# The opening of a two-block transformer kernel: the order of its modulation units, first key blocks and context squares

## The chip, the cores and the metric

The kernel runs on one core of a Trainium2 chip. The core has five engines that run their own programs and wait for each other through semaphores: TensorE (PE: matmuls; its weight loads are shown apart as PEld), VectorE (DVE), ScalarE (ACT), GpSimd (POOL) and SyncE (SP, which here issues every DMA but one). The metric is the device time of one execution in microseconds (us); lower is better.

## What is computed

The reference applies a first block of two layers (a grouped-query attention layer with a context, then a neighbourhood attention layer), and a second block (an mLSTM branch and a sparse attention branch, merged). The change touches the start of the first layer alone:

```python
mod_x = (silu_c @ w_mod[i] + b_mod[i])[:, None, :]
mod_c = silu_cc @ w_mod[i] + b_mod[i]
sh_x, sc_x, g_x = jnp.split(mod_x, 3, axis=-1)
sh_c, sc_c, g_c = jnp.split(mod_c, 3, axis=-1)
hx = rms_norm(x, norm_g[i]) * (1.0 + sc_x) + sh_x
hc = rms_norm(ctx, norm_g[i]) * (1.0 + sc_c) + sh_c
...
k = px[..., A_WIDTH:A_WIDTH + A_KV_WIDTH].reshape(b, t, A_KV_HEADS, HEAD_DIM)
pkv = hc @ w_in[:, A_WIDTH:A_WIDTH + 2 * A_KV_WIDTH]
```

x has 512 tokens and ctx 256, both of width 1024. Everything is float32 and is kept to near that precision: each operand of a projection is split into a high part and a low part (its rest), and each product is three matmuls (high by high, high by low, low by high).

## The kernel before

**Layout.** Activations lie transposed, in eight blocks of 128 features (k = 0 to 7): 512 columns of x and 256 of the context each. HX and LX are the high and low parts of x after norm and modulation, HC and LC those of the context, WH and WL those of the weights. Weights come in units of 1 MB; a unit has four quarters of 512 columns, and quarter q serves the blocks k = 2q and 2q + 1.

**Order.** A Python list, `plan`, is filled in program order by `do(...)`. Every engine then walks the same list and emits its own share of each item, so each engine runs strictly in the list's order, and moving a line in the opening moves it on all engines at once. There is no scheduler in the part that is changed; the order is written by hand, and `opening[0] = True` keeps the projections from putting weight splits between themselves.

**Modulation units.** Shift and scale of the first layer come from eight units, 0 to 3 (shift) and 4 to 7 (scale). `EARLY` gives their order of loading: 0, 4, 1, 5, 2, 6, 3, 7; this text calls them e0 to e7 in that order, and `first[n]` is the generator of en. `next(first[n])` puts three things into the list: the 8 matmuls of the unit (`mod_mm`, L1722, 16 in the trace), and ACT's copy of their sum out of PSUM (`mod_row`, L1998). `run(first[n])` puts the rest: two transposes on PE (`mod_tr`, L1730) and the small DVE operations (L2276 to L2285) that make the shift, or for e1, e3, e5 and e7 the gain. e(2j) and e(2j+1) together serve the blocks k = 2j and 2j + 1. Four buffers hold the loaded units: the load of e(n+4) waits for the matmuls of en (L2882).

**Per block of x.** `scale(k)` is DVE's product of x, gain and norm factor (L2327, into AR) and then ACT's addition of the shift, rounded to HX (L2022). `scale_low(k)` is DVE's rest, LX (L2333). `keys_rows(0, [k])` is the six matmuls of 512 columns of block k (L1704 to L1706). They wait for LX of that block and the WL quarter.

**Context.** `square("a", k, 1)` squares block k of the context on ACT (L2009) and adds it on DVE (L2294); `norm_sums` sums over the partitions on PE (L1740); `norm_rs` is DVE's mean (L2300) and POOL's power (L2763); `rbroad` is DVE's diagonal (L2315) and PE's broadcast (L1747); `scale_ctx` is ACT's copy of the broadcast factors, Rc (L2015). From there `ctx_normed(k)` is POOL's product with Rc (L2775), `ctx_rows_in(k)` is two ACT operations (L2030, HC, and L2032, the same in full) and POOL's rest LC (L2780), and `keys_rows(1, ks)` the matmuls of 256 columns on the context's blocks.

**Weight splits.** `tick(True)` puts one quarter's split into the list: ACT's cast to WH (L1991) and POOL's rest WL (L2756), or DVE's (L2268) for unit 1. After the fourth quarter follows the load of the unit after next.

**Fillers.** `busy(n)` issues n matmuls on constants into an unused bank (L1713, two passes each in the trace). Their result is read by nobody.

Of the kernel before, what the change touches and what calls it, by code (L numbers as in the profile page):

```python
# [172 lines left out]
def build(nc, wu, vp, cc, cs1, xt, biasb, pos, out):  # L173
    ctx = ExitStack()
    with ctx:
# [152 lines left out]
        def do(*item):  # L328
            plan.append(item)
            done_work[0] += COST.get(item[0], 0)  # L330
# [12 lines left out]
        def run(g):  # L343
            for _ in g:
                pass
# [5 lines left out]
        def load(n):  # L351
            if n < len(UNITS):
                loaded.add(n)
                loaded_at[n] = done_work[0]
                do("load", n)
# [8 lines left out]
        def tick(forced=False):  # L364


            if opening[0] and not forced:
                return
            if pieces and (forced or not careful[0] or done_work[0] - loaded_at[pieces[0][0]] > 9):
                n, q = pieces.pop(0)  # L370
                split_by[n, q] = "pool" if n != 1 and not quick[0] else "dve"
                do("split", n, q)
                if q == 3:
                    load(n + 2)
                split_ready()

        def split_ready():
            for m in sorted(loaded):
                if UNITS[m][0] not in PLAIN and m not in started and part_last[PART[m]] in (None, *unit_end):
                    split(m)  # L380
# [29 lines left out]
        def pj(key, un, lo, hi, f0, phase, o, ks=range(8), half=None):  # L410

            groups[key] = Group(key, un.n, False, lo, hi, f0, 128, phase, o, half)
            for k in ks:
                if k % 4 == 3:
                    tick()
                do("proj", key, k)
                yield (hi - lo) / (100 if half is None else 200)
# [35 lines left out]
        def early_unit(n, pr):  # L453
            w = early[n % 4].rearrange("p (k f) -> p k f", k=8)
            return mod_unit(0, EARLY[n], pr, w, (s_early[n % 4], (n,)), lambda: None)
# [35 lines left out]
        def rbroad(name, p, o):  # L491
            rbout[name, p] = o
            for i in range(*norms[name].parts[p]):
                dg_prev[name, i], dg_last[i % 4] = dg_last[i % 4], (name, i)
                do("rbroad", name, i)
# [53 lines left out]
        first = [early_unit(n, FIRST if n < 2 else MODS) for n in range(8)]  # L549
        modulate(0, PS[:, 0:1024], "a", False, hb0, "a", ())  # L550

        def keys_rows(j, ks):
            lo, hi = FULL[j]
            for m in range(2):
                run(pj(("ak", m, j), un, lo, hi, 128 * m, "a", K4[m][:, lo:hi], ks))

        def ctx_rows_in(*ks):
            for k in ks:
                do("low_ctx_k", 0, k)

        def ctx_normed(*ks):
            for k in ks:
                do("norm_ctx_k", 0, k)

        def scale(*ks):
            for k in ks:
                do("scale", 0, k)

        def scale_low(*ks):
            for k in ks:  # L570
                do("scale_low", 0, k)
# [20 lines left out]
        tick(True)  # L592
        scale(0, 1)
        scale_low(0, 1)
        do("busy", 3)
        next(first[2])
        do("busy", 3)
        tick(True)
        for k in range(4, 8):
            do("square", "a", k, 1)  # L600
        keys_rows(0, [0])
        next(first[3])
        keys_rows(0, [1])
        tick(True)
        tick(True)
        run(first[2])
        run(first[3])
        do("norm_sums", "a", 1)
        do("norm_rs", "a", 1)

        next(first[4])
        scale(2, 3)
        next(first[5])
        rbroad("a", 1, PS[:, 0:1024])
        do("scale_ctx", 0)
        ctx_normed(0, 1, 2, 3)
        scale_low(2, 3)
        run(first[4])
        run(first[5])
        keys_rows(0, [2, 3])  # L620
        ctx_rows_in(0, 1)

        scale(4)
        next(first[6])
        scale(5)
        next(first[7])
        ctx_normed(4, 5)
        scale_low(4, 5)
        keys_rows(0, [4])
        run(first[6])  # L630
        run(first[7])
        ctx_rows_in(2, 3)
        keys_rows(0, [5])
        keys_rows(1, [0, 1])

        scale(6, 7)
        ctx_normed(6, 7)
        scale_low(6, 7)
        opening[0] = False
# [536 lines left out]
        first = [(s_post, ("b", 31)), (s_gated, ("b", 7))]  # L1176
# [301 lines left out]
        def hidden(m, blocks, pr):  # L1478

            un = Unit("w1" + "kv"[m])  # L1480
            w1[m] = (un.n, bank(pr.take(("w1", m), (s_hid, (m,)))))
            for i, n in enumerate(blocks):
                for x in range(n):
                    do("n_hidden", m, sum(blocks[:i]) + x)
                yield
            un.done(s_hidp, m)
# [47 lines left out]
        hv, first = hidden(1, [0, 0, 0] + [2] * 8, SEVEN), first_probs()  # L1534
# [1566 lines left out]
```

## Time and profile before

| | us |
|---|---|
| median of 3 executions | 1564.93 |
| their range | 1561.18 to 5181.44 |
| the profiled execution | 1565.51 |
| its span in the trace | 1563.5 |

| engine | busy us | share of the span |
|---|---|---|
| PE | 1512.9 | 97% |
| PE weight loads | 1226.5 | 78% |
| DVE | 755.4 | 48% |
| POOL | 688.3 | 44% |
| ACT | 645.7 | 41% |

Times in the trace count from the start of the span. A line of the timeline gives the start, the busy time of the instructions merged into it, the engine, the source line, what is written and read, the shapes and the count; in brackets how long the engine was idle before it and what released it. A busy PE is not PE at its peak, since matmuls are pipelined and their ends are modelled. The first 60 us are the stage of the change.

### The profile page before, as it was taken

What the parts mean: (1) busy time and instruction counts of PE and PEld (TensorE: products, weight loads), DVE (VectorE), ACT (ScalarE), POOL (GpSimd) and SP (SyncE); (2) the same over time, 40 slices, a digit from 0 to 9 for tenths busy, and PEclk for the clock granted to TensorE, in tenths of its full rate; (3) what the DMA queues carried; (4) which work ended last, traced back from release to release, by engine and by line L of the source; (5) the groups of instructions that cost most, each with busy time, mean ns of one, the idle gap of its engine ahead of it and who ended that gap; (6) DMA issues with size and microseconds to landing.
All of it is one profiled execution on the core that took longest, in us unless ns stands there. A gap on an engine that the chain in (4) does not pass through costs nothing.

```text
span 1563.5 us, 25447 instructions
## 1 busy us (share of the span) xinstructions
PE 1512.9 (97%) x10072; PEld 1226.5 (78%) x10072; DVE 755.4 (48%) x1675; ACT 645.7 (41%) x1393; POOL 688.3 (44%) x661
## 2 busy tenths in 40 slices
PE   7999999999899999999998999999999999999997
PEld 4877777777687888787876896878787877777887
DVE  5344545445534344435455765734443564555154
ACT  5345444444532533333334553445333334444331
POOL 3444444444532533433434535445355435554462
PEclk9999999999999999999999999999999999999999
DMA  9211111121033222322221322122131231111221
GB/s 394 77 55 55 55 55 37 56 72 54 1 109 108 82 81 82 108 82 82 85 105 34 129 88 81 59 87 98 54 108 55 85 105 55 54 55 55 84 91 67
DMA packets 23285, 128.22 MB, mean 82 GB/s; under 512 B 2432, under 2 KB 4736, under 8 KB 9216
## 3 DMA queue, kind: packets, MB, share of 16 engines
q1 hardware_dynamic: 23024, 126.35, 23.0%
q8 instruction: 80, 1.31, 0.3%
q10 hardware_dynamic: 144, 0.26, 0.1%
q14 instruction: 37, 0.30, 0.1%
HBM read 124.50 MB, written 2.10 MB: 81 GB/s over the span
## 4 chain that ended last, share of the span: by engine, by line
PE 85%; DVE 4%; ACT 4%; POOL 3%; issue 2%; DMA 1%; SPq 0%; POOLq 0%; DVEq 0%; ACTq 0%
PE PS L1704 17%; PE PS L1706 16%; PE PS L1705 16%; PE PS L1800 7%; PE PS L1790 7%; PE PS L1826 6%; PE PS L1696 3%; PE PS L1697 3%; PE PS L1698 3%; POOL WL L2756 1%; PE PS L1722 1%; PE PS L1883 1%; PE PS L1875 1%; DVE sm L2416 1%; ACT WH L1991 1%
## 5 line engine op out<-in xcount | busy, mean ns | idle before, releaser
L2756 POOL TENSOR_TENSOR WL<-W,WH 128x512 fp32r<-128x512 f32 x307 | 411.1, 1353 | 329.5 <-ACT WH L1991 329.4
L1704 PE MATMUL PS<-HX,WH 128*128 128x512 f32 (+1 forms) x1032 | 414.3, 401 | 8.0 <-POOL WL L2756 5.1
L1706 PE MATMUL PS<-HX,WL 128*128 128x512 f32 (+1 forms) x1032 | 393.5, 381 | 0.0
L1705 PE MATMUL PS<-LX,WH 128*128 128x512 f32 (+1 forms) x1032 | 393.5, 381 | 0.0
L1704 PEld LDWEIGHTS PS<-HX,WH 128*128 128x128 f32 x1032 | 196.2, 190 | 55.0 <-issue 17.5
L1706 PEld LDWEIGHTS PS<-HX,WL 128*128 128x128 f32 x1032 | 195.8, 190 | 38.5
L1705 PEld LDWEIGHTS PS<-LX,WH 128*128 128x128 f32 x1032 | 196.6, 191 | 32.3 <-issue 2.6
L2815 POOL TENSOR_SCALAR AR<-AR,sm 128x768 f32<-128x768 f32 (+4 forms) x160 | 112.6, 708 | 248.1 <-DVE sm L2435 246.4
L1991 ACT CAST WH<-W 128x512 fp32r<-128x512 f32 x320 | 187.9, 621 | 36.9 <-DMA W<-in_wu 13.6
L2416 DVE TENSOR_REDUCE sm<-PS 128x1 f32<-128x512 f32 (+4 forms) x192 | 145.0, 755 | 55.1 <-PE PS L1790 51.2
L2077 ACT ACTIVATE AR<-PS,sm 128x768 f32<-128x768 f32 (+4 forms) x160 | 114.9, 722 | 104.3 <-DVE sm L2421 86.1
L2088 ACT COPY AR<-PS 128x512 f32<-128x512 f32 (+1 forms) x112 | 62.2, 555 | 154.3 <-PE PS L1800 154.1
L1790 PE MATMUL PS<-AR 64*128 64x256 f32 (+3 forms) x704 | 119.1, 453 | 4.7 <-ACT AR L2077 1.7
L2815 POOL TENSOR_SCALAR XC<-XC,sm 128x512 f32<-128x512 f32 x64 | 45.3, 708 | 160.4 <-DVE sm L2435 160.4
L1704 PE MATMUL PS<-HC,WH 128*128 128x256 f32 (+1 forms) x344 | 108.8, 316 | 1.0 <-POOL LC L2780 1.0
L2077 ACT ACTIVATE XC<-PS,sm 128x512 f32<-128x512 f32 x64 | 44.1, 690 | 146.1 <-DVE sm L2421 146.1
L1706 PE MATMUL PS<-HC,WL 128*128 128x256 f32 (+1 forms) x344 | 103.3, 300 | 0.0
L1800 PE MATMUL PS<-C,AR 128*128 128x128 f32 x608 | 95.7, 281 | 4.4 <-DVE AR L2455 3.1
L1790 PEld LDWEIGHTS PS<-AR 64*128 64x128 f32 x704 | 59.6, 186 | 49.4 <-issue 38.1
L1826 PEld LDWEIGHTS PS<-AR 128*64 128x64 f32 x1408 | 76.2, 137 | 28.2 <-issue 24.7
L1826 PE MATMUL PS<-AR 128*64 128x128 f32 x1408 | 93.6, 279 | 4.3 <-DVE AR L2444 2.5
L1696 PE MATMUL PS<-WH,HX 128*128 128x256 f32 x320 | 94.0, 294 | 0.0
(284 smaller groups left out, 2507.1 us busy)
## 6 DMA issues: line engine op xcount, KB each, us to landing
W<-in_wu SPq DMA_DIRECT2D x98, 1024.0 KB, 4.8
AR<-in_wu SPq DMA_DIRECT2D x8, 1024.0 KB, 10.0
AR<-in_biasb SPq DMA_DIRECT2D x32, 256.0 KB, 2.8
XX<-in_xt SPq DMA_DIRECT2D x2, 1024.0 KB, 6.3
XC<-in_xt SPq DMA_DIRECT2D x1, 1024.0 KB, 12.8
out<-XX SPq DMA_DIRECT2D x2, 512.0 KB, 3.0
out<-XX SPq DMA_DIRECT2D x4, 256.0 KB, 2.2
C<-in_cc SPq DMA_DIRECT2D x1, 642.5 KB, 11.1
```

The lines of the kernel that those rows point to most:

```text
L1696: e.matmul(o, xh, wh, start=(k == 0), stop=False)
L1704: e.matmul(o, wh, xh, start=(k == 0), stop=False)
L1705: e.matmul(o, wh, xl, start=False, stop=False)
L1706: t = e.matmul(o, wl, xh, start=False, stop=(k == 7))
L1790: t = e.matmul(PS[:, s.score[h] + a:s.score[h] + b], l, r, start=True, stop=True)
L1800: t = e.transpose(o[:, j * 128:j * 128 + 128], s.pb[h][:, (q0 + j) * 128:(q0 + j) * 128 + 128], c("id"))
L1826: t = e.matmul(s.out[h][j], s.values[h][j], s.pt[h][:, j * 128:j * 128 + 128], start=(j % apart == 0 and s.first), stop=(j % apart == apar ...
L1991: e.copy(WH[:, PART[n], a:z], W[:, n % 2, a:z]).then_inc(*s_wh.by(n, q))
L2077: t = e.activation(s.pb[h][:, a:b], PS[:, s.score[h] + a:s.score[h] + b], ACT.Exp, bias=smn[:, i % 4, g:g + 1], scale=(1.0 if s.scale is N ...
L2416: e.tensor_reduce(mx, x, AX.X, ALU.max).then_inc(*s_max.by(name, n, h))
L2756: e.tensor_tensor(WL[:, d, a:z], W[:, n % 2, a:z], WH[:, d, a:z].bitcast(F32), ALU.subtract).then_inc(*s_wl_pool.by(n, q))
L2815: t = e.tensor_scalar(x, x, rin[:, i % 8, g:g + 1], 1.0 if s.gate is None else s.gate[h][:, g:g + 1], ALU.mult, ALU.mult)
```

## The change

The two groups of three fillers behind the first modulation units go. The matmuls of e3 move ahead of block 0's keys, and the transposes of e2 and e3 between the keys of block 0 and block 1. Squares of context blocks 6 and 7 move behind `scale(2, 3)`. e4 and e5 are multiplied ahead of block 2's keys, and transposed behind them. The context's sums, its power, its broadcast and Rc move behind the keys of blocks 2 and 3. Of the context's blocks, 0 and 1 are brought in between the matmuls of e6 and e7, 2 and 3 behind `scale(6, 7)`.

```diff
--- before.py
+++ after.py
@@ -592,48 +592,46 @@
         tick(True)
         scale(0, 1)
         scale_low(0, 1)
-        do("busy", 3)
         next(first[2])
-        do("busy", 3)
         tick(True)
-        for k in range(4, 8):
+        for k in range(4, 6):
             do("square", "a", k, 1)
+        next(first[3])
         keys_rows(0, [0])
-        next(first[3])
+        run(first[2])
+        run(first[3])
         keys_rows(0, [1])
+        next(first[4])
+        scale(2, 3)
+        for k in range(6, 8):
+            do("square", "a", k, 1)
+        next(first[5])
+        scale_low(2, 3)
         tick(True)
         tick(True)
-        run(first[2])
-        run(first[3])
+        keys_rows(0, [2])
+        run(first[4])
+        run(first[5])
         do("norm_sums", "a", 1)
+        keys_rows(0, [3])
+        scale(4)
         do("norm_rs", "a", 1)
-
-        next(first[4])
-        scale(2, 3)
-        next(first[5])
+        scale(5)
         rbroad("a", 1, PS[:, 0:1024])
         do("scale_ctx", 0)
         ctx_normed(0, 1, 2, 3)
-        scale_low(2, 3)
-        run(first[4])
-        run(first[5])
-        keys_rows(0, [2, 3])
+        next(first[6])
+        scale_low(4, 5)
         ctx_rows_in(0, 1)
-
-        scale(4)
-        next(first[6])
-        scale(5)
         next(first[7])
-        ctx_normed(4, 5)
-        scale_low(4, 5)
         keys_rows(0, [4])
         run(first[6])
         run(first[7])
+        ctx_normed(4, 5)
+        keys_rows(0, [5])
+        scale(6, 7)
         ctx_rows_in(2, 3)
-        keys_rows(0, [5])
         keys_rows(1, [0, 1])
-
-        scale(6, 7)
         ctx_normed(6, 7)
         scale_low(6, 7)
         opening[0] = False
```

Source lines below the change are two lower in the changed kernel (L1998 is L1996 there). The rows below are the programs of the engines in their order, each with the semaphores it waits for.

PE, from behind the transposes of e0 and e1, before: L1713 are fillers, L1722 the modulation matmuls, L1704 to L1706 the keys.

```order
L1713 MATMUL PS<-C 128x256 x3
L1722 MATMUL PS<-AR,sm 32x256 [waits early2,norm_var]
L1722 MATMUL PS<-AR,sm 32x256 x7
L1713 MATMUL PS<-C 128x256 x3
L1704 MATMUL PS<-HX,WH 128x512 [waits x_low_dve,w_low_pool,mod_gain]
L1705 MATMUL PS<-LX,WH 128x512
L1706 MATMUL PS<-HX,WL 128x512
L1704 MATMUL PS<-HX,WH 128x512
L1705 MATMUL PS<-LX,WH 128x512
L1706 MATMUL PS<-HX,WL 128x512
L1722 MATMUL PS<-AR,sm 32x256 [waits early3,mod]
L1722 MATMUL PS<-AR,sm 32x256 x7
```

The same place in the changed kernel, where L1720 are the modulation matmuls, L1702 to L1704 the keys and L1728 the transposes.

```order
L1720 MATMUL PS<-AR,sm 32x256 [waits early2,norm_var]
L1720 MATMUL PS<-AR,sm 32x256 x7
L1720 MATMUL PS<-AR,sm 32x256 [waits early3,mod]
L1720 MATMUL PS<-AR,sm 32x256 x7
L1702 MATMUL PS<-HX,WH 128x512 [waits x_low_dve,w_low_pool,mod_gain]
L1703 MATMUL PS<-LX,WH 128x512
L1704 MATMUL PS<-HX,WL 128x512
L1702 MATMUL PS<-HX,WH 128x512
L1703 MATMUL PS<-LX,WH 128x512
L1704 MATMUL PS<-HX,WL 128x512
L1728 MATMUL PS<-C,AR 128x128 [waits mod_row]
L1728 MATMUL PS<-C,AR 128x128
```

e3's matmuls stand ahead of the first six key matmuls instead of behind them, the transposes of e2 and e3 right behind these instead of behind twelve, and the fillers are gone.

ACT, from behind the cast of unit 0's second quarter, before: L2009 are squares of the context, L1998 the copies of modulation sums, L1991 the casts, L2022 the blocks of HX, L2015 is Rc.

```order
L2009 ACTIVATE AR<-XC 128x256 [waits squares_added] x4
L1998 COPY AR<-PS 128x256 [waits mod_turned,mod_sums]
L1991 CAST WH<-W 128x512 x2
L1998 COPY AR<-PS 128x256 [waits mod_turned,mod_sums]
L2022 ACTIVATE HX<-AR,sm 128x512 [waits mod,scaled]
L2022 ACTIVATE HX<-AR,sm 128x512 [waits scaled]
L1998 COPY AR<-PS 128x256 [waits mod_turned,mod_sums]
L2015 COPY AR<-PS 128x256 [waits rs_broad]
```

The same place in the changed kernel (L2020 is HX, L1989 the cast, L2013 Rc).

```order
L2007 ACTIVATE AR<-XC 128x256 [waits squares_added] x2
L1996 COPY AR<-PS 128x256 [waits mod_turned,mod_sums] x2
L2020 ACTIVATE HX<-AR,sm 128x512 [waits mod,scaled]
L2020 ACTIVATE HX<-AR,sm 128x512 [waits scaled]
L2007 ACTIVATE AR<-XC 128x256 [waits squares_added] x2
L1996 COPY AR<-PS 128x256 [waits mod_turned,mod_sums]
L1989 CAST WH<-W 128x512 x2
L2020 ACTIVATE HX<-AR,sm 128x512 [waits mod,scaled]
L2020 ACTIVATE HX<-AR,sm 128x512 [waits scaled]
L2013 COPY AR<-PS 128x256 [waits rs_broad]
```

The copies of e3's and e4's sums (the "x2") now stand directly ahead of HX of blocks 2 and 3; the squares of blocks 6 and 7, the copy of e5's sums and both casts stand behind it; HX of blocks 4 and 5 stands ahead of Rc. On DVE the additions of squares 6 and 7 stand, in the same way, between the products of blocks 2 and 3 and their LX.

ACT, from HX of block 4 on, before; a pair of L2030 and L2032 is one block of the context.

```order
L2022 ACTIVATE HX<-AR,sm 128x512 [waits mod,scaled]
L1998 COPY AR<-PS 128x256 [waits mod_turned,mod_sums]
L2022 ACTIVATE HX<-AR,sm 128x512 [waits scaled]
L1998 COPY AR<-PS 128x256 [waits mod_turned,mod_sums]
L2030 ACTIVATE HC<-AR,sm 128x256 [waits normed_ctx,mod_gain]
L2032 ACTIVATE AR<-AR,sm 128x256 [waits x_high]
L2030 ACTIVATE HC<-AR,sm 128x256 [waits normed_ctx]
L2032 ACTIVATE AR<-AR,sm 128x256 [waits x_high]
L2022 ACTIVATE HX<-AR,sm 128x512 [waits mod,scaled]
L2022 ACTIVATE HX<-AR,sm 128x512 [waits scaled]
L2030 ACTIVATE HC<-AR,sm 128x256 [waits normed_ctx,mod_gain]
L2032 ACTIVATE AR<-AR,sm 128x256 [waits x_high]
```

The changed kernel, from the copy of e7's sums on (L2020 is HX of blocks 6 and 7 here, L2028 and L2030 a block of the context).

```order
L1996 COPY AR<-PS 128x256 [waits mod_turned,mod_sums]
L2020 ACTIVATE HX<-AR,sm 128x512 [waits mod,scaled]
L2020 ACTIVATE HX<-AR,sm 128x512 [waits scaled]
L2028 ACTIVATE HC<-AR,sm 128x256 [waits normed_ctx,mod_gain]
L2030 ACTIVATE AR<-AR,sm 128x256 [waits x_high]
L2028 ACTIVATE HC<-AR,sm 128x256 [waits normed_ctx]
L2030 ACTIVATE AR<-AR,sm 128x256 [waits x_high]
L2028 ACTIVATE HC<-AR,sm 128x256 [waits normed_ctx,mod_gain]
L2030 ACTIVATE AR<-AR,sm 128x256 [waits x_high]
L2028 ACTIVATE HC<-AR,sm 128x256 [waits normed_ctx]
L2030 ACTIVATE AR<-AR,sm 128x256 [waits x_high]
```

Ahead of HX of blocks 6 and 7 before stood four blocks of the context, now two; behind it, until the last block, four before and six now.

## Rows read from the trace of the kernel before

**Rows 1.** Page: busy us, share and instructions of each engine.
```profile
PE 1512.9 (97%) x10072; PEld 1226.5 (78%) x10072; DVE 755.4 (48%) x1675; ACT 645.7 (41%) x1393; POOL 688.3 (44%) x661
```

**Rows 2.** PE in order of time, 21 to 53 us.
```profile
21.88 1.07 PE L1722 MATMUL PS<-AR,sm 128*32 128x256 f32 x16
...
26.35 1.07 PE L1722 MATMUL PS<-AR,sm 128*32 128x256 f32 x16
...
28.87 0.60 PE L1730 MATMUL PS<-C,AR 128*128 128x128 f32 x4
...
29.74 1.93 PE L1722 MATMUL PS<-AR,sm 128*32 128x256 f32 x32
32.30 0.71 PE L1747 MATMUL PS<-AR,C 128*128 128x128 f32 x4 [0.63 <-DVE AR L2315]
...
52.52 0.28 PE L1696 MATMUL PS<-WH,HX 128*128 128x256 f32 x1
```

**Rows 3.** ACT in order of time, 25 to 44 us.
```profile
25.16 0.72 ACT L2009 ACTIVATE AR<-XC 128x256 f32<-128x256 f32 x2
...
30.88 0.37 ACT L1998 COPY AR<-PS 128x256 f32<-128x256 f32 x1 [1.69 <-PE PS L1722]
31.14 1.33 ACT L2022 ACTIVATE HX<-AR,sm 128x512 fp32r<-128x512 f32 x2
...
33.05 0.37 ACT L2015 COPY AR<-PS 128x256 f32<-128x256 f32 x1 [0.31 <-PE PS L1747]
34.45 0.60 ACT L2030 ACTIVATE HC<-AR,sm 128x256 fp32r<-128x256 f32 x1 [1.03 <-POOL AR L2775]
...
36.72 0.71 ACT L2022 ACTIVATE HX<-AR,sm 128x512 fp32r<-128x512 f32 x1
...
42.12 1.38 ACT L2022 ACTIVATE HX<-AR,sm 128x512 fp32r<-128x512 f32 x2 [1.27 <-DVE AR L2327]
```

**Rows 4.** POOL in order of time, 31 to 50 us.
```profile
31.20 0.72 POOL L2763 TENSOR_TENSOR sm<-sm 128x2 f32<-128x2 f32 x1
33.50 2.96 POOL L2775 TENSOR_TENSOR AR<-XC,AR 128x256 f32<-128x256 f32 x4 [1.57 <-ACT AR L2015]
...
49.13 0.74 POOL L2780 TENSOR_TENSOR LC<-AR,HC 128x256 fp32r<-128x256 f32 x1 [0.40 <-ACT AR L2032]
```

**Rows 5.** DMA issues from 4.9 to 5.4 us; then all weight loads to 60 us.
```profile
AR<-in_wu SPq DMA_DIRECT2D x1, 1024.0 KB, 16.8
```
```profile
DMA to landing us min/median/max: 4.8/10.1/18.8
```

**Rows 6.** DVE in order of time, 25 to 42 us.
```profile
25.61 2.89 DVE L2294 TENSOR_TENSOR AR<-AR 128x256 f32<-128x256 f32 x4 [0.27 <-ACT AR L2009]
...
30.19 1.41 DVE L2327 SCALAR_TENSOR_TENSOR AR<-XX,sm,PS 128x512 f32<-128x512 f32 x2
31.96 0.48 DVE L2315 TENSOR_SCALAR AR<-C,sm 128x128 f32<-128x128 f32 x2 [0.36 <-POOL sm L2763]
32.35 1.41 DVE L2333 SCALAR_TENSOR_TENSOR LX<-AR,sm,HX 128x512 fp32r<-128x512 f32 x2
...
41.34 1.41 DVE L2327 SCALAR_TENSOR_TENSOR AR<-XX,sm,PS 128x512 f32<-128x512 f32 x2
```

**Rows 7.** SP's queue: the issue of unit 2's load.
```profile
31.35 0.33 SPq L2892 DMA_DIRECT2D W<-in_wu  x1
```

**Rows 8.** Groups of PE's instructions by shape, 20.2 to 33 us: the fillers.
```profile
L1713 PE MATMUL PS<-C 128*128 128x256 f32 x12 | 3.0, 388 | 0.0
```

**Rows 9.** Windows of all engines: busy us of PE, PEld, DVE, ACT, POOL, granted clock, DMA.
```profile
503.50:504.00 0.50, 0.00 (x0) 0.00 (x0) 0.50 (x2) 0.00 (x0) 0.00 (x0) 0.50 1.13 475
...
504.30:510.00 5.70, 5.70 (x16) 4.62 (x16) 4.07 (x5) 3.97 (x8) 3.00 (x5) 0.50 0.14 57
```

**Rows 10.** Window of PE alone: busy us, granted clock, DMA.
```profile
834.00:835.00 1.00, 0.66 (x7) 0.70 0.00 0
```

**Rows 11.** PE in order of time, at 504 us.
```profile
504.27 1.23 PE L1747 MATMUL PS<-AR,C 128*128 128x128 f32 x4 [2.52 <-DVE AR L2315]
```

## The prediction, written before the changed kernel was run

> **What bounds the kernel now.** I read the page first: PE is busy 97% of the span [rows 1], so what counts in a stage is when PE gets its operands. The change lies wholly ahead of 52.5 us, where the keys end and the next unit's matmuls start [rows 2]. Nothing behind it waits for a fixed time, since every later load is released by work; so I take what the keys' end moves by as what the whole moves by, and ask only for that. Next the timelines of the engines. Before, four things set the keys' end, in turn: the landing of the modulation units (e2 is issued at 5.0 and lands 16.8 later, at 21.8; its matmuls start at 21.88) [rows 2, 5]; the chain from e3's transposes to HX of blocks 2 and 3; Rc at 33.05; and from there ACT, which is hardly idle from 34.45 on and brings in eight context blocks, four HX, two copies and two casts, until the last LC is ready at 49.13 + 0.74 = 49.87 [rows 3, 4]. PE then needs 2.65 us more. I follow the changed order along the same chain, with durations of before.
>
> **e3 earlier (the gain).** e3 is the fourth unit, issued 0.4 behind e2, and has the longest landing of all, 18.8 [rows 5]: it is there at 24.2. Its matmuls take 1.07 [rows 2], so 24.2 to 25.3; before they started at 26.35, behind block 0. That is 2.1 us. Block 0 follows, to 26.8 (a block of six matmuls takes 28.87 - 27.42 = 1.45 [rows 2]), then the transposes of e2 and e3 at 26.8 instead of 28.87. From there to DVE's product of block 2 it is 30.19 - 28.87 = 1.3 [rows 2, 6]: 28.1. DVE has squares 4 and 5 to add first, from 25.61; all four took 2.89 [rows 6], two of them until about 27.4, which makes it 28.4, and 29.8 for both products. So far 1.8 us ahead.
>
> **The fillers.** They are 12 passes, 3.0 us of PE [rows 8], in a stretch in which PE waits for e2 and for LX anyway. Their time is worth nothing; what they covered is below.
>
> **Where the lead goes.** PE: transposes 0.4, block 1 to 28.6, e4 to 29.6, e5 to 30.6. ACT has the copy of e4's sums in front of HX of block 2, so HX waits for PE: the copy 29.65 to 30.0, HX of 2 and 3 (1.33) to 31.3, squares 6 and 7 (0.72) to 31.95 [rows 3]. Before, HX started at 31.14; the lead is down to 1.1. On DVE the additions 6 and 7 stand ahead of LX and cannot end before 32.6; LX of block 2 is 32.65 to 33.4 (1.41 for two, it started at 32.35 before [rows 6]). PE, idle since 30.6, starts block 2 at 33.5. Before, it was there at 33.2, behind the broadcast and with all transposes done: the lead is gone, and 1.7 us of small PE work (0.87 for transposes and sums, 0.71 for the broadcast [rows 2]) still to do.
>
> **Rc.** Block 2 to 34.95, transposes of e4 and e5, sums, block 3 to 37.3. DVE's products of 4 and 5 start 1.3 behind the transposes, at 36.2, with the mean between them, to 37.9. POOL's power waits for the mean, 37.15 to 37.9 (0.72 [rows 4]); the diagonals 0.48 from 37.95 [rows 6]; the broadcast from 38.3; Rc 0.75 behind its start, as 33.05 stands to 32.30 [rows 2, 3]: 39.05. That is **6.0 us later** than before.
>
> **The context chain.** POOL's first product is ready at 40.35 (33.50 is 0.45 behind Rc and HC starts 0.95 after it [rows 3, 4]), and ACT has the copy of e6's sums (matmuls 38.9 to 39.9) done by 40.3: HC of block 0 at 40.4 instead of 34.45. Blocks 0 and 1 take 36.72 - 34.45 = 2.27 [rows 3], to 42.7, and the copy of e7's sums stands behind them: 43.05. PE has done block 4 by 42.3 and waits with e7's transposes until then. 1.15 later is the product of block 6 (0.2 less than for a pair of units), 44.2; HX of block 6 is 42.12 - 41.34 = 0.8 behind it [rows 3, 6]: 44.95 to 45.0, before 42.12. From HX of block 6 to the last LC it took 49.87 - 42.12 = 7.75; now two more context blocks stand in between, 2.27. The last LC is ready at 44.95 + 7.75 + 2.27 = 54.97, **5.1 us later**, and with it the keys' end, 57.6.
>
> What hides nothing: POOL's other work (16 operations of 0.74) would be done by 51.3 from Rc on, so ACT bounds. What stays hidden: the casts of unit 0's last quarters go from ahead of e4's copy to behind e5's, about 4 us later, and with them POOL's splits (to 36) and SP's load of unit 2, issued at 31.35 before [rows 7] and now near 36. A load lands within 18.8 [rows 5], so by 55 at worst; its casts stand behind the keys' end. The quarters themselves are wanted by block 4 at 40.8. SP's load of e7 goes out 2.1 us earlier and is wanted at 39.9. If these covers failed they would cost at most the 2 us between 55 and 57.6.
>
> **The clock.** Here the trace says more than the sum of durations. After a wait of 2.52 us at 501.8 to 504.3 [rows 11] the granted clock is 0.50, so 1.2 GHz instead of 2.4, for the 5.7 us to 510, while PE works throughout [rows 9]. At 834 us it falls in a stretch in which PE is not idle for long but only 0.66 us busy in each [rows 10]. The changed opening has three such stretches: 20.4 to 24.2, where only e2's 1.07 us are left and the fillers gone; 30.6 to 33.5, idle; and 49.5 to 55, where PE has four pieces of a third of a us, each behind one LC. Before, none of them is there. The Trainium skill, page "TensorE: Matmul & The Clock Gate", section on the clock gate, says that throttled is the default state and activity releases it; by that the fillers are what holds the clock, and the rule speaks against this change; rows 9 to 11 agree. What it costs, from both sides: nothing, if the clock holds; in the second stretch block 2 and its transposes run at half speed on the path, 1.45 + 0.4 = 1.9; in the third, PE runs behind the last LC without a wait, and half of up to 5.7 us is 2.9, less what of the low time passes while it waits; I take 2.0. In the first, e3, block 0, transposes, block 1 and e4 would take twice as long: 1.07 + 1.45 + 0.4 + 1.45 + 1.0 = 5.4. I take the second and third, since there PE does next to nothing, and leave the first out, since e2 and the end of the first transposes lie in it.
>
> **The sum.** 5.1 + 1.9 + 2.0 = 9.0 us on the profiled execution's 1565.5 gives 1574.5. That execution is 0.6 us above the median shown, 1564.9; I say **1574**.
>
> **The rivals.**
> - *The clock holds.* For it: the stretches of before with waits of 0.4 to 0.6 us left the blocks at 1.45 us each. Then only the context chain is late: 1565.5 + 5.1 = 1570.6.
> - *The clock is low from the start.* For it: without the fillers PE has one unit's matmuls between two waits there, as thin a stretch as that at 834 [rows 10]. Then 9.0 + 5.4: 1580.
> - *The other side: not slower.* The keys are paced by the modulation units, and the context chain gives its lateness back. It would need HX of block 6 to start by 39.85 (42.12 less the 2.27 of two blocks behind it), 5.1 before my time, so ACT would have to be free of the two waits I give it, for e4's matmuls at 29.6 and for Rc at 39.05. Then at most the 2.1 us of e3 stay: 1563.4. Against it: Rc stands behind block 3 in PE's program, whatever the durations are, and block 3 behind squares 6 and 7.
>
> **How the numbers follow.** Chain late and clock low in two stretches: 0.42. Clock holds: 0.23. Low from the start: 0.18. Not slower: 0.15. The rest, 0.02, is something outside these. The range goes from 1564, which cuts off most of the last rival, to 1582, which is the third case with 2 us for the executions' own scatter (1561.2 and 1564.9 for the same kernel). About 2%, 31 us, is what a measurement of this kernel can tell from no change; the whole stage is 52.5 us long, and none of the cases comes to half of that. So faster by more than 2% gets 0.01, slower 0.02, within 0.97.
>
> **What would show it.** Right: e3's matmuls near 24.2; HX of block 2 right behind a copy that waited for PE; block 2 at 33 to 34; Rc near 39; the last LC near 55; PE's first matmul of the next unit at 57 to 61; low granted clock, or blocks of 2.6 to 2.9 us, between 31 and 40 and from 52 on. Wrong: Rc before 36, or the last LC before 52, breaks the chain; all blocks at 1.45 breaks the clock's term. A keys' end that is late while the total isn't would break the step that the rest of the kernel moves along.

## The result, and the profile after

The changed kernel took 1575.91 us, the median of four executions (1571.90 to 1576.21); the kernel before took 1565.32 beside it. The ratio is **1.0071, 95% interval 1.0055 to 1.0088**: slower by about 11 us, and within 2%. The 1565.32 is the median of four executions, one of which took 5181.44 us and is left out of the ratio, as is one of 2476 us of run a4 below. The prediction was 1574, in a range of 1564 to 1582. The profiled execution is the fastest of the four, 1571.90, with a span of 1569.9 against 1563.5 before; the other three took 1575.9 to 1576.2, with a lower mean granted clock (0.986 against 0.990).

The page's engine row of the changed kernel (busy us, share, instructions) says as little about the opening as that of before did [rows 1]:

```profile
PE 1512.6 (96%) x10060; PEld 1226.4 (78%) x10060; DVE 756.4 (48%) x1675; ACT 645.7 (41%) x1393; POOL 688.8 (44%) x661
```

The engines' timelines do, in order of time. PE, 21 to 60 us, as [rows 2]:

```profile
21.45 1.07 PE L1720 MATMUL PS<-AR,sm 128*32 128x256 f32 x16 [1.39 <-DMA AR<-in_wu]
23.93 1.07 PE L1720 MATMUL PS<-AR,sm 128*32 128x256 f32 x16 [1.41 <-DMA AR<-in_wu]
...
28.35 1.93 PE L1720 MATMUL PS<-AR,sm 128*32 128x256 f32 x32
33.19 0.47 PE L1702 MATMUL PS<-HX,WH 128*128 128x512 f32 x1 [2.91 <-DVE LX L2331]
...
42.78 0.44 PE L1728 MATMUL PS<-C,AR 128*128 128x128 f32 x2 [0.43 <-ACT AR L1996]
...
54.71 0.58 PE L1702 MATMUL PS<-HC,WH 128*128 128x256 f32 x1
...
59.30 0.28 PE L1694 MATMUL PS<-WH,HX 128*128 128x256 f32 x1
```

ACT, as [rows 3]:

```profile
29.49 0.37 ACT L1996 COPY AR<-PS 128x256 f32<-128x256 f32 x1 [3.73 <-PE PS L1720]
29.76 1.33 ACT L2020 ACTIVATE HX<-AR,sm 128x512 fp32r<-128x512 f32 x2
31.00 0.71 ACT L2007 ACTIVATE AR<-XC 128x256 f32<-128x256 f32 x2
...
38.71 0.37 ACT L2013 COPY AR<-PS 128x256 f32<-128x256 f32 x1 [0.50 <-PE PS L1745]
40.11 0.60 ACT L2028 ACTIVATE HC<-AR,sm 128x256 fp32r<-128x256 f32 x1
...
44.66 1.38 ACT L2020 ACTIVATE HX<-AR,sm 128x512 fp32r<-128x512 f32 x2 [1.93 <-DVE AR L2325]
```

POOL and DVE, as [rows 4, 6]: the last split pair and the last LC, and DVE's work between 31 and 35 us.

```profile
32.56 3.31 POOL L2754 TENSOR_TENSOR WL<-W,WH 128x512 fp32r<-128x512 f32 x2 [6.32 <-ACT WH L1989]
...
53.91 0.75 POOL L2778 TENSOR_TENSOR LC<-AR,HC 128x256 fp32r<-128x256 f32 x1 [0.39 <-ACT AR L2030]
```
```profile
31.43 0.95 DVE L2292 TENSOR_TENSOR AR<-AR 128x256 f32<-128x256 f32 x2 [2.16 <-ACT AR L2007]
32.30 2.43 DVE L2331 SCALAR_TENSOR_TENSOR LX<-AR,sm,HX 128x512 fp32r<-128x512 f32 x2
```

What is to be seen: e3 starts 2.4 us earlier (23.93, before 26.35); 0.4 of that is an earlier start of this execution (e2 at 21.45, before 21.88), which stands in all times below. ACT then does nothing for 3.73 us until e4's matmuls let it copy, and HX of block 2 follows right behind, 1.4 earlier. Squares and additions push LX to 32.30, and block 2 starts at 33.19 against 33.24: the lead is spent. Rc is at 38.71 against 33.05, HX of block 6 at 44.66 against 42.12, the last LC ready at 54.66 against 49.87. So far the chain. Behind it PE needs 4.6 us to the next unit (54.66 to 59.30), where it needed 2.65. The windows of PE of the changed kernel say why (length, busy us, granted clock, DMA):

```profile
48.00:52.00 4.00, 2.71 (x16) 1.00 0.01 2
52.00:56.00 4.00, 3.30 (x12) 0.55 0.00 0
56.00:60.00 4.00, 4.00 (x23) 0.60 0.75 260
60.00:64.00 4.00, 4.00 (x36) 1.00 0.01 2
```

The clock falls near 52.4 us to its lower level, 1.2 GHz, after a stretch in which PE had one context block at a time, and rises near 59. Between 18.3 us, where the clock's record begins (last section), and 60 us it falls only there. The keys' end moved by 59.30 - 52.52 = 6.8 us, and the span by 6.4.

### The profile page after: what moved, and what is told of

Its sections match the earlier page's. It is cut to its first block, busy times and chain, and to the rows that moved or that the text cites. A ratio compares the mean times of both kernels' runs of the same rounds, so it can differ in the third digit from the quotient of the medians.

```text
span 1569.9 us, 25423 instructions
## 1 busy us (share of the span) xinstructions
PE 1512.6 (96%) x10060; PEld 1226.4 (78%) x10060; DVE 756.4 (48%) x1675; ACT 645.7 (41%) x1393; POOL 688.8 (44%) x661
## 4 chain that ended last, share of the span: by engine, by line
PE 85%; DVE 4%; ACT 4%; POOL 3%; issue 2%; DMA 1%; SPq 0%; POOLq 0%; DVEq 0%; ACTq 0%
PE PS L1702 17%; PE PS L1704 16%; PE PS L1703 16%; PE PS L1798 7%; PE PS L1788 7%; PE PS L1824 6%; PE PS L1694 3%; PE PS L1696 3%; PE PS L1695 3%; PE PS L1720 1%; DMA AR<-in_wu 1%; POOL WL L2754 1%; PE PS L1881 1%; PE PS L1873 1%; DVE sm L2414 1%
## 5 line engine op out<-in xcount | busy, mean ns | idle before, releaser
L1702 PE MATMUL PS<-HX,WH 128*128 128x512 f32 (+1 forms) x1032 | 414.5, 402 | 10.9 <-POOL WL L2754 5.9
L1704 PE MATMUL PS<-HX,WL 128*128 128x512 f32 (+1 forms) x1032 | 393.6, 381 | 0.0
L1702 PEld LDWEIGHTS PS<-HX,WH 128*128 128x128 f32 x1032 | 196.0, 190 | 58.0 <-issue 19.6
L1704 PEld LDWEIGHTS PS<-HX,WL 128*128 128x128 f32 x1032 | 195.7, 190 | 38.1
L1989 ACT CAST WH<-W 128x512 fp32r<-128x512 f32 x320 | 187.8, 621 | 37.0 <-DMA W<-in_wu 13.7
L1702 PE MATMUL PS<-HC,WH 128*128 128x256 f32 (+1 forms) x344 | 110.6, 321 | 2.0 <-POOL LC L2778 1.9
L1704 PE MATMUL PS<-HC,WL 128*128 128x256 f32 (+1 forms) x344 | 104.6, 304 | 0.0
```

What stands on the lines that cost most here:

```text
L1702: e.matmul(o, wh, xh, start=(k == 0), stop=False)
L1704: t = e.matmul(o, wl, xh, start=False, stop=(k == 7))
L1989: e.copy(WH[:, PART[n], a:z], W[:, n % 2, a:z]).then_inc(*s_wh.by(n, q))
```

## The experiments

Each was timed in five rounds beside the kernel before. The whole-kernel times mix two things, the chain and the clock, so the table takes them apart. Every execution has its time and its mean granted clock; within one kernel the time falls by 0.92 us for each 0.001 of clock (one slope for 179 executions of 14 groups, rest 0.9 us). "At equal clock" is the difference to before after that slope is taken off, with about ±0.6 to ±0.9. It is an estimate: it counts low clock at its mean price, and where PE waits anyway the clock costs less. The ± is the scatter alone; that the column can be off by about 2 us more shows in a4, whose traced chain is nearly that of before and which comes out at -2.4.

| run | ratio, 95% | mean us against before | mean clock (before) | at equal clock | last LC | keys' end |
|---|---|---|---|---|---|---|
| a1_again | 1.0075, 1.0063–1.0088 | +9.6 | .9881 (.9921) | +6.0 | 54.81 | 59.44 |
| a2_fillers_back | 1.0052, 1.0039–1.0065 | +7.6 | .9896 (.9921) | +5.4 | 54.76 | 57.42 |
| a3_fillers_late | 1.0049, 1.0037–1.0062 | +7.2 | .9893 (.9921) | +4.7 | 58.07 | 60.73 |
| b1_fillers_all | 1.0035, 1.0022–1.0048 | +5.5 | .9920 (.9912) | +6.2 | 55.10 | 57.77 |
| b2_squares_ahead | 1.0023, 1.0015–1.0031 | +3.7 | .9925 (.9912) | +4.9 | 53.60 | 56.28 |
| b3_factors_ahead | 1.0004, 0.9996–1.0013 | +0.6 | .9931 (.9912) | +2.3 | 51.86 | 54.53 |
| b4_e3_alone | 0.9998, 0.9989–1.0006 | -0.4 | .9915 (.9912) | -0.2 | 49.26 | 51.92 |
| a4_before_no_fillers | 1.0008, 0.9998–1.0019 | +1.2 | .9882 (.9921) | -2.4 | 49.19 | 51.85 |
| c1_turn_first | 0.9994, 0.9985–1.0004 | -1.0 | .9914 (.9922) | -1.7 | 48.01 | 50.68 |
| c2_turn_and_e3 | 0.9994, 0.9984–1.0005 | -0.9 | .9903 (.9922) | -2.6 | 48.75 | 51.43 |
| c3_turn_e3_late_fillers | 1.0005, 0.9993–1.0016 | +0.5 | .9918 (.9922) | +0.2 | 49.16 | 53.17 |

The last two columns are from each run's one profiled execution (before: 49.87 and 52.52); a few tenths of them are its start. "From e2" below is such a time less the start of e2's matmuls in the same trace, which takes the execution's own start out: the last LC is 28.0 from e2 before, and 33.2 in both traces of the changed kernel.

### The changed kernel once more, and its clock

**a1_again** is the changed kernel without an edit.

> The changed kernel once more, with a second trace. Its four executions came to 1571.9 once and to 1575.9 to 1576.2 three times, with a mean granted clock of 0.990 and 0.986. If the difference is the clock (theory 1), the share of executions near 1576 stays high, their granted clock is lower than that of those near 1572, and a trace of one near 1576 shows one more stretch at 0.50 than the trace of 1571.9 does, 4 us of loss. If it is something else, such as a DMA that lands later (theory 2), the granted clock of the two groups is the same in the traces. Ratio to the kernel before 1.005 to 1.009 by both.

The median was 1574.86 against 1564.6. Its trace is that of the first profile within 0.2 us: last LC 54.81, low clock from 52.5 to 59.3, keys' end 59.44. The profiled execution was a fast one again (1568.54, clock 0.992), so the two theories are parted by the mean clock alone: of the eleven executions of both runs, seven took 1574.2 to 1576.6 us with a clock of 0.986, and none of these has a trace. Where their clock was low is not shown. And without any fit: two of its executions had a mean clock of 0.992 and took 1569.9; nine of before at 0.992 took 1564.7. At the same mean clock the change costs 5.2 us. (The first of the two is the traced one: it has the fall in the third stretch, and less low clock behind 800 us than the traced execution of before.)

**a2_fillers_back** puts both groups of fillers back.

```diff
+        do("busy", 3)
         next(first[2])
+        do("busy", 3)
         tick(True)
```

> The changed order with both groups of three fillers back around e2's matmuls, nothing else. The chain theory (the context's factors and blocks are late) has nothing here: keys' end as in the changed kernel, total 1.005 to 1.007 of before. The clock theory in its first stretch: if the missing fillers let the clock fall between 20 and 24 us in part of the executions, the executions near 1576 become those near 1572, so about 3 to 5 us less in the median than the changed kernel. If the fillers delay e3, 0 to 0.5 us more.

The median was 1572.07, 2.8 us less than a1. The chain did not move (last LC 54.76). The two groups stand between 20 and 24 us, and PE was busy for 3.84 of these 4 us instead of 1.25. In the profiled execution no fall came before 66 us, not even in the thin last stretch, where the fillers do nothing; that is this execution's luck, not theirs, since PE was as thin there as in a1.

**a3_fillers_late** leaves the opening as changed and puts five fillers between the last context blocks.

```diff
                 if k % 4 == 3:
                     tick()
+                if key == ("ak", 0, 1) and k in (4, 5, 6, 7):
+                    do("busy3", {4: 2, 5: 1, 6: 1, 7: 1}[k])
                 do("proj", key, k)
```

`busy3(n)` is `busy(n)` into another bank; its definition is left out here.

> The changed kernel with five fillers (2.4 us of PE) in the gaps between the last context blocks of the keys, 50 to 55 us, in a bank that is free there. Clock theory: PE is kept busy there, the granted clock doesn't fall at 52.7 us, the last 4.6 us of keys behind the last LC take 2.65 again, so the keys' end comes 2.0 us earlier and the total is 2 us lower than the changed kernel. Rival: the clock falls all the same and the fillers delay blocks: 0 to 1 us slower than the changed kernel.

The median was 1570.93, 3.9 less than a1. In the trace PE needs 2.66 us behind the last LC, as before, at 2.4 GHz. One trace doesn't show that the fillers did this, since a2's clock held there without them; but with late fillers it held in that stretch in all four traces of this order (a3, b1, b2, b3), without them in one of three. The expected gain was 2 us. But this execution shows the other two stretches of the prediction, which neither a1 nor the first profile had. PE's windows of a3:

```profile
20.00:24.00 4.00, 1.93 (x16) 0.57 1.00 418
24.00:28.00 4.00, 3.69 (x22) 0.58 1.03 426
28.00:32.00 4.00, 4.00 (x44) 1.00 1.01 418
32.00:36.00 4.00, 1.09 (x7) 0.77 0.99 414
36.00:40.00 4.00, 4.00 (x15) 0.50 0.93 322
```

and PE's timeline of a3 in the second of them:

```profile
34.98 0.77 PE L1704 MATMUL PS<-HX,WH 128*128 128x512 f32 x1 [2.91 <-DVE LX L2338]
...
37.68 1.06 PE L1735 MATMUL PS<-C,AR 128*128 128x128 f32 x4
...
39.24 0.77 PE L1704 MATMUL PS<-HX,WH 128*128 128x512 f32 x1
```

From block 2 to block 3 it takes 4.26 us here and 35.46 - 33.19 = 2.27 in the changed kernel's first trace: 2.0 for a fall in the second stretch. With a fall in the first, block 2 starts at 34.98 instead of 33.19; 0.4 of these 1.8 us are a later start (e2 at 21.82 instead of 21.45), so the fall costs 1.4. Together they put the last LC at 58.07, 3.4 behind that of the first trace and 3.0 later from e2. So all three stretches can fall, and which of them does differs between executions of one opening. No trace has the pair that was forecast, the second and the third. The Trainium skill, page "TensorE: Matmul & The Clock Gate", section "What's actually happening", says that the gate's observation runs freely and isn't tied to the kernel's start; these traces agree with that.

**b1_fillers_all** has the fillers of a2 and of a3, and five more (`do("busy", 5)`) ahead of block 2's keys, so in all three stretches.

> The changed order with fillers in all three thin stretches: the six of before around e2, five ahead of block 2's keys, five between the last context blocks. Theory (late chain plus clock): no fall of the granted clock before 60 us in any trace, keys' end 2.65 us behind the last LC, last LC still at 54.7 to 55, so total 1564.6 + 5.1 = 1569.7, ratio 1.003 to 1.004, executions close together. Rival (the clock is all of it): ratio 1.000. Rival (fillers only get in the way): 1.005 or more.

The ratio fell to 1.0035, +5.5 us in the mean, with a clock (0.9920) as high as that of before; the trace shows none below 1.00 until 900 us. Its windows of PE:

```profile
48.00:52.00 4.00, 3.69 (x21) 1.00 0.01 2
52.00:56.00 4.00, 3.71 (x22) 1.00 0.00 0
56.00:60.00 4.00, 4.00 (x36) 1.00 0.70 217
```

The last LC is as late as in the changed kernel, 55.10. This parts the loss, without the fit: 5 to 6 us are the chain, and about 4 (9.6 less 5.5), which the fillers take away, the clock.

**a4_before_no_fillers** takes the two groups from the kernel before.

```diff
-        do("busy", 3)
         next(first[2])
-        do("busy", 3)
```

> The kernel before without its two groups of fillers, order unchanged. If the fillers only pass time: 0.0 to 0.3 us less than before. If they hold the clock: the granted clock falls between 22 and 26 us, the first key blocks take 2.6 to 2.9 us each instead of 1.45, and the keys' end is 2 to 5 us later, ratio 1.001 to 1.003. This gives the price of the fillers apart from the order.

1.0008, interval 0.9998 to 1.0019. The mean clock fell by 0.004, as much as in the changed kernel, yet the time rose by only 1.2 us. The trace shows a fall between 21.4 and 24.8:

```profile
20.00:24.00 4.00, 2.30 (x17) 0.67 1.02 424
24.00:28.00 4.00, 4.00 (x28) 0.90 1.03 426
```

PE waits for e2 and for LX in that stretch, and the keys' end is not later for it (51.85, before 52.52), so half speed is cheap there; the expected 2 to 5 us did not come. (The trace is again of one of the faster executions, 1564.61 with a clock of 0.991; the mean of a4 is 0.988.) That explains a part of the 2.4 us "at equal clock" at most; the rest of it is open.

### The chain, part by part

**b2_squares_ahead** is b1 with squares 6 and 7 ahead of block 0's keys (and two fillers instead of five ahead of block 2).

```diff
         next(first[3])
+        for k in range(6, 8):
+            do("square", "a", k, 1)
         keys_rows(0, [0])
...
         scale(2, 3)
-        for k in range(6, 8):
-            do("square", "a", k, 1)
         next(first[5])
```

> As b1_fillers_all, but squares 6 and 7 of the context go back ahead of block 0's keys (behind e3's copy), so that DVE no longer has two additions between the products of blocks 2 and 3 and their LX; two fillers instead of five ahead of block 2. Chain theory: block 2 starts at 31.6 instead of 33.5, everything behind it 1.9 us earlier, last LC 53.1, ratio to before 1.002. If the squares' place is harmless: last LC 54.7 to 55 as in b1.

Against b1 the median fell by 1.9 us, the last LC by 1.5. DVE has its operands for LX earlier, in b2:

```profile
30.74 1.41 DVE L2341 SCALAR_TENSOR_TENSOR LX<-AR,sm,HX 128x512 fp32r<-128x512 f32 x2 [1.43 <-ACT HX L2030]
```

and block 2 starts at 32.03 instead of 33.53. Its LX was ready at 31.49; the two fillers held PE for the other 0.5 us. So two squares in the wrong gap cost 1.5 to 1.9 us.

**b3_factors_ahead** is b2 with sums, power, broadcast, Rc and the first context products back ahead of block 2, and with them the two weight splits; the two fillers ahead of block 2 are gone. `ctx_rows_in(0, 1)` stays behind `scale(4)` and `scale(5)`.

```diff
         keys_rows(0, [1])
+        tick(True)
+        tick(True)
+        do("norm_sums", "a", 1)
+        do("norm_rs", "a", 1)
         next(first[4])
         scale(2, 3)
         next(first[5])
+        rbroad("a", 1, PS[:, 0:1024])
+        do("scale_ctx", 0)
+        ctx_normed(0, 1, 2, 3)
         scale_low(2, 3)
-        tick(True)
-        tick(True)
-        do("busy", 2)
         keys_rows(0, [2])
         run(first[4])
         run(first[5])
-        do("norm_sums", "a", 1)
         keys_rows(0, [3])
         scale(4)
-        do("norm_rs", "a", 1)
         scale(5)
-        rbroad("a", 1, PS[:, 0:1024])
-        do("scale_ctx", 0)
-        ctx_normed(0, 1, 2, 3)
```

> As b2_squares_ahead, and the context's sums, power, broadcast, Rc and first four products go back to their place of before, ahead of block 2's keys; the order of what ACT does behind that (HX of 4 and 5, e6's copy, two context blocks, e7's copy, HX of 6 and 7, six context blocks) stays that of the changed kernel. Rc at 32.8 instead of 38.7. If the late Rc is what costs (as the prediction put it): last LC near 50, ratio 1.000 to 1.001. If it is ACT's order behind Rc that costs: HX of 6 at 42.9, last LC at 52.9, no better than b2, ratio 1.002.

Rc came 5.7 us earlier than in b2, at 31.99, 1.1 earlier than before. The last LC came only 1.7 earlier. ACT's timeline of b3:

```profile
31.99 0.38 ACT L2022 COPY AR<-PS 128x256 f32<-128x256 f32 x1
35.77 1.38 ACT L2029 ACTIVATE HX<-AR,sm 128x512 fp32r<-128x512 f32 x2 [3.41 <-DVE AR L2334]
...
41.86 1.38 ACT L2029 ACTIVATE HX<-AR,sm 128x512 fp32r<-128x512 f32 x2 [1.93 <-DVE AR L2334]
```

ACT stands still for 3.41 us at HX of block 4, with the context's first products ready: these blocks are queued behind it. Before, ACT did two of them in that gap and two more ahead of HX of block 6 [rows 3]. So it isn't Rc's lateness alone that costs, but the context work that stands behind HX of blocks 4 and 6 in ACT's order. I had expected 52.9 for the last LC; it was 51.86, between the two theories. Counted from e2, the last LC stands at 33.2 in the changed kernel, 32.0 in b2, 30.0 in b3 and 28.0 before: of the chain's 5.2 us, 1.2 are the squares (1.4 against b1), 2.0 Rc and what moved with it, and 2.0 what is left. That these are ACT's order is read from its queue; no run puts that order back alone. The ratio, 1.0004, flatters b3: its clock was the highest of all (0.9931), at equal clock it is 2.3 us slower, as its keys' end (+2.0) says.

**b4_e3_alone** is the kernel before with only the part that was to gain: e3's matmuls ahead of block 0, the transposes ahead of block 1, squares 6 and 7 right behind e3.

```diff
-        for k in range(4, 8):
+        for k in range(4, 6):
             do("square", "a", k, 1)
-        keys_rows(0, [0])
         next(first[3])
-        keys_rows(0, [1])
-        tick(True)
-        tick(True)
+        for k in range(6, 8):
+            do("square", "a", k, 1)
+        keys_rows(0, [0])
         run(first[2])
         run(first[3])
+        keys_rows(0, [1])
+        tick(True)
+        tick(True)
```

> The kernel before with e3 alone moved: its matmuls ahead of block 0's keys, its copy between squares 5 and 6, the transposes of e2 and e3 between blocks 0 and 1. All else, the fillers too, as before. The lead of 2.1 us at e3's matmuls should be eaten by what stands behind it (e4 waits for block 1 and the sums, POOL's splits hold its power until 31.0): Rc 0.3 us earlier, last LC 49.5 to 49.9, ratio 0.999 to 1.000. If the modulation units pace the opening: 1.5 to 2 us earlier, ratio 0.9988.

0.9998, interval 0.9989 to 1.0006: nothing. e3 starts at 24.02, but HX of block 2 only at 30.18 (before 31.14), and HX of block 6 at 41.51 (before 42.12). Of a lead of 2.3 us 0.6 is left at the last LC; 0.35 of both is this execution's earlier start (e2 at 21.53), so of 2.0 about 0.3 is left, which is no more than the scatter of one trace.

### Does anything here beat the kernel before?

In the kernel before, ACT waits 1.27 us for block 6's product [rows 3], since e6's and e7's transposes stand behind block 4's keys. **c1_turn_first** moves them ahead of these.

```diff
-        keys_rows(0, [4])
         run(first[6])
         run(first[7])
+        keys_rows(0, [4])
```

> The kernel before, with one edit: the transposes of e6 and e7 stand ahead of block 4's keys instead of behind them; everything else, the fillers too, is as before. In the kernel before PE does these transposes at 40.01, behind block 4's keys, and ACT is then idle for 1.27 us ahead of HX of block 6 (42.12). The copy of e7's sums is done at 38.6, so the transposes can start there, 1.4 earlier. Theory (the chain behind the last pair of modulation units sets ACT's order to the end, lateness there passes to the keys' end one for one): HX of block 6 starts where ACT is free of its two context blocks, at about 40.9 to 41.2, the last LC is ready at 48.7 to 49.0 instead of 49.87, the keys' end is near 51.5, and the whole gives a ratio of 0.9992 to 0.9995. Rival (later stages give such a lead back, as they did with the 0.6 us of the run in which e3 alone was moved): the keys' end earlier by about 1 us but a ratio of 1.0000 or more.

ACT's timeline of c1:

```profile
40.26 1.38 ACT L2022 ACTIVATE HX<-AR,sm 128x512 fp32r<-128x512 f32 x2 [0.28 <-DVE AR L2327]
```

The idle time is 0.28 instead of 1.27, the edit's 1.0 us as expected; the keys' end came 1.8 earlier. The other 0.8 was there already at HX of block 4 (35.86, before 36.72), behind an earlier block 0 (24.11, before 24.82) that the edit doesn't touch. At equal clock c1 is 1.7 us faster (±0.6, and see a4 for what that is worth), in time 0.9994 with an interval to 1.0004. It has the lowest median of the study, and is not shown to be faster than before.

**c2_turn_and_e3** adds b4's edit to c1's; **c3_turn_e3_late_fillers** adds the late fillers of a3 to that.

> The kernel before with two edits: e3's matmuls and the transposes of e2 and e3 as in the changed kernel (squares 6 and 7 right behind e3), and the transposes of e6 and e7 ahead of block 4's keys. Context factors, Rc, the context's blocks and the fillers as before. Theory: the leads add, as each lies on the chain: 0.6 us from e3 alone and 1.0 from the transposes; HX of block 6 at 40.3 to 40.6, last LC ready at 48.2 to 48.5, ratio 0.9988 to 0.9992. Rival: nothing reaches the total, 0.9998 to 1.0004.

> The kernel of the run before this one, and five fillers between the last context blocks' keys. Fillers cost PE nothing there, as it waits for LC. In the kernel before the granted clock stays at full in that stretch, with a PE about as thin, so theory: same time as the run before within 0.6 us. Rival (the clock does fall there in some executions of the kernel before as well): 1 us less in the median, and less scatter.

c2 gave 0.9994 too, short of the 0.9988 to 0.9992 expected. Its trace starts like that of before (e2 at 21.96), and its last LC is 1.1 us earlier: the 1.0 of the transposes and what little b4 had left of e3's lead. So the leads do add in the trace, and are too small for the time to tell. c3 was 1.8 us slower than c2 in the median, and my expectation that fillers are free there fell. PE's timeline of c3:

```profile
47.44 1.02 PE L1722 MATMUL PS<-C 128*128 128x256 f32 x4
48.11 0.47 PE L1708 MATMUL PS<-HC,WH 128*128 128x256 f32 x1
...
53.17 0.28 PE L1700 MATMUL PS<-WH,HX 128*128 128x256 f32 x1
```

The last LC is ready at 49.16, and PE needs 4.0 us from there, at full clock. In this order PE is nearly full at the end of the keys (c2 waits 0.50 us once), so the fillers' passes push real work back. In the changed kernel's order, where PE waits for each block, the same five cost nothing (2.66 behind the last LC in a3).

c3's trace shows one thing more. It has the first two groups of fillers, as before, and its clock falls all the same, from 23.0 to 26.4 us. PE's timeline and windows of c3:

```profile
17.27 1.46 PE L1717 MATMUL PS<-C 128*128 128x256 f32 x6
21.53 1.07 PE L1731 MATMUL PS<-AR,sm 128*32 128x256 f32 x16 [2.79 <-DMA AR<-in_wu]
22.53 2.51 PE L1717 MATMUL PS<-C 128*128 128x256 f32 x6
```
```profile
20.00:24.00 4.00, 2.47 (x21) 0.87 1.02 424
24.00:28.00 4.00, 4.00 (x25) 0.70 1.01 422
```

In this execution PE reached the first group at 17.27 (before: 20.27) and had spent it long before e2 landed. Fillers run as soon as PE comes to them, so they cover a wait only when it begins about then. In b1 and c1 PE waited 2.6 us for e2 in the same way, and the clock held; so even this is not certain.

## Why the prediction was right

**The chain, 5.1 us.** Step by step, predicted and then measured in the changed kernel's first trace: e3's matmuls 24.2, 23.93; HX of block 2 30.0, 29.76, behind e4's copy; block 2 33.5, 33.19, waiting for LX; Rc 39.05, 38.71; first HC 40.4, 40.11; e7's transposes wait for ACT's copy until 43.05, 42.78; HX of block 6 44.95, 44.66; last LC 54.97, 54.66. Each is 0.2 to 0.35 early by one and the same offset: in this trace everything starts 0.4 earlier (e2 at 21.45 instead of 21.88). Set against that, the last LC is 5.2 later than before. For the whole, a1 at one mean clock gives 5.2, b1 +5.5, and the runs at equal clock with this chain 4.7 to 6.2. The parts hold less well. I laid most of the loss at the late Rc; if that were so, b3 with Rc back in its place should have had its last LC near 50. It gained 2.0 us of the 4.0 then left; the other 2.0 stand with the order of ACT's work behind Rc. b2 shows the squares' share, and b4 that the lead of e3 is gone by itself. Two of my sums are off by 0.1: the small PE work left before Rc is 0.87 + 0.71 = 1.6, not 1.7, and the first product 39.05 + 0.45 + 0.95 = 40.45, not 40.35; neither set anything.

**The clock, 1.9 + 2.0 us.** The term for the third stretch was 2.0; both traces of the changed kernel show 59.30 - 54.66 - 2.65 = 2.0 and 59.44 - 54.81 - 2.65 = 2.0. The term for the second was 1.9; a3 shows 2.0, but the other traces of the same opening (the first profile, a1, a2) show no fall there. It was sized rightly (1.7 of the 2.0 are left at e6's matmuls) and is paid by only some executions. For the first stretch I named 5.4 if the clock is low from the start, and left it out. It does fall in a3, but rises again in the middle of block 0, which makes 1.4. "Before, none of them is there" was too strong: c3, with the fillers of before, falls in the first. Over all executions of a1 the clock's share is 9.6 - 6.0 = 3.6 us by the fit, or 9.6 - 5.2 = 4.4 by its executions at one clock; my sum had 3.9. That it came out so close is in part luck: no trace has the two falls that I added, one term paid in some executions stood for another that was left out, and the seven executions near 1576 have no trace to say which falls they paid.

**The rest of the kernel** moves along, as I took it to. Counted back from the end of the program, ACT's instructions near 60 us are 6.8 us later in the changed kernel's first trace than before, and those near 800 us 6.7. In a1 it is 6.9 near 60 and 7.1 near 600, but 3.1 at the end: behind 800 us the trace of before has 17 us of low clock (ahead of the last 10 us), a1's has 7. Such differences between executions are as large as a term of my sum, so the total of one trace tests none of them.

**The covers** held. The splits of unit 0's last quarters ended at 35.87 (predicted 36), its successor's load was issued at 35.96, and nothing behind the keys waited for it.

**What I did not foresee.** LX of blocks 2 and 3 took 2.43 us together instead of 1.41 [rows 6], because POOL's splits now run beside them. Block 2 waits for the first one alone, which was as fast as ever, so it cost nothing.

**The rivals.** Not slower: excluded, the context chain gives none of its lateness back. Clock holds: true of a2's trace to 66 us and of b1's, and the time it gave, 5.1 above, is what b1 measured (+5.5). Low from the start: 1580 was too much, going by a3, the one trace of this order with a fall there, since the clock comes back sooner.

## What to carry to other kernels

On an engine that runs in list order, a lead ends at the next foreign wait in its queue: e3 came 2 us earlier and ACT spent that behind a copy that waited for e4. Move work behind a wait only when nothing needed later is queued behind it. And where an order leaves TensorE with one small piece at a time, count the clock as its own term, per stretch, and expect only some executions to pay it; fillers help where PE truly waits, cost where it doesn't (1.3 us at c3's keys' end), and are spent before the wait when PE comes to them early.

## What the runs showed of the hardware

**VectorE and GpSimd side by side.** Of the two LX in the changed kernel the first took 0.745 us and the second, beside POOL's split, 1.772; POOL's pair of splits took 3.31 instead of 2.52. The additions of two SBUF operands show the same in the kernel before (DVE instructions of 25 to 29 us: shortest, median, longest in ns; the longest is the one beside a split of POOL):

```profile
L2294 DVE TENSOR_TENSOR AR<-AR x4: 425/426/1298, 25.6 to 28.1; 128x256 f32<-128x256 f32 x4
```

DVE's products with an operand in PSUM stay at 0.74 to 0.75 beside POOL's work (41.3 to 42.7 us in the kernel before). The Trainium skill, page "SBUF — State Buffer", section "SBUF: two separate sides", says that a DVE operation with two SBUF inputs and a GpSimd operation that reads SBUF exclude each other for a whole instruction; the rows agree with it in which of DVE's operations are hit, and the slow addition ends 0.28 us behind POOL's split (26.90 and 26.62).

**Where the granted clock's record begins.** The windows show 1.00 from the start of the span, yet e0's and e1's 32 matmuls, from 15.45 us on, took 3.47 us in the kernel before, and 1.93 in a4. The trace's record of the clock has no entry until the clock first rises to 2.4 GHz, at 18.61 us in the kernel before and at 14.52 in a4, and a window without an entry is shown as 1.00. So a 1.00 ahead of that point says nothing, and the low time there is missing in the mean clock too. In the thirteen traces the first entry lies between 12.8 and 14.7 us or between 18.2 and 18.7. Of the changed order with fillers in at most one stretch, the three traces with the late one (the first profile, a1, a2) fell in the third stretch or in none, and a3, with the early one (13.71), in the first and second: its PE reached e2 sooner and waited 3.73 us for it instead of 1.39. That this decides which stretches fall is not shown; four traces are few. An early rise also moves block 0: c1, whose program is that of before up to there, rises at 13.54 and starts it at 24.11 instead of 24.82.
